# The order of ScalarE's work in each step of an expert loop, and the place of SiLU's table load

## The chip, the cores and the metric

The kernel runs on one core of a Trainium2 chip. The metric is the device time in microseconds (us) from start to end of one execution; lower is better. Engines are named as in the profile: PE is TensorE's matmuls, PEld its weight loads, DVE is VectorE, ACT is ScalarE, POOL is GpSimd, SP is SyncE, which issues the loads of weights.

## The reference

A model of 256 tokens of width 1024 in fp32. First come two hybrid layers, then two layers that mix pooling and attention; the first of these ends in a dense SwiGLU, the second in a mixture of 8 experts. The change lies in the experts:

```python
def swiglu(h, wg, wu, wd):
    return (jax.nn.silu(h @ wg) * (h @ wu)) @ wd

def moe_swiglu(h, w_router, wg, wu, wd):
    xt = h.reshape(-1, D)
    logits = (xt @ w_router).astype(jnp.float32)
    top_v, top_i = lax.top_k(logits, TOP_K)
    gates = jax.nn.softmax(top_v, axis=-1)
    gate = jnp.sum(jax.nn.one_hot(top_i, N_EXPERTS) * gates[..., None], axis=1)
    y = jnp.zeros_like(xt)
    for e in range(N_EXPERTS):
        y = y + gate[:, e:e + 1] * swiglu(xt, wg[e], wu[e], wd[e])
```

wg and wu are 1024 x 3584 for each expert, wd is 3584 x 1024. A final rmsnorm follows.

## The kernel before, in words

**Split products.** An fp32 weight is used as two numbers that TensorE multiplies faster, a high part and a low part. SyncE loads a chunk of weights of 1 MiB (128 x 2048 fp32) into one of 6 buffers `raw`. ScalarE copies it to `whi` (the high part, two instructions of 128x1024, function `act_hi_moe`). VectorE subtracts, `wlo = raw - whi` (`dve_lo_moe`, two instructions). TensorE then multiplies with both. There are 4 buffers `whi` (`HIGH`), 3 buffers `wlo` (`SPLIT`) and 6 `raw` (`RAW`). A `raw` buffer is free once its low part is made (`lo_ready`), and SyncE waits for that before it issues the load of the chunk six places on.

**Jobs, pairs and steps.** Tokens are gathered by expert into jobs. The kernel works on pairs of jobs: a heavy one (up to 128 tokens) and a light one (up to 64, its high and low parts side by side). A job has 42 chunks: for each block of 1024 columns 4 chunks of the gate's weights (`g`) and 4 of the value's (`u`), three times, then a block of 512 columns with 2 and 2, then 14 chunks of the down weights (`d`). A pair so has 84 steps, one chunk each, in an order written out by hand (`FIRST_ORDER` for the first pair, 12 steps of the heavy job alone, then heavy and light by turns; `PAIR_ORDER` for the others). Four pairs run here, three written out and one in a loop with a trip count from the router. A heavy step is 12 matmuls of 128x512, a light one 8.

**What a step asks of ScalarE.** At step `i` it makes the high part of chunk `i + 4`, which may start when TensorE has finished step `i` (`split_used`) and the chunk has landed. At some steps it also reads accumulators out of PSUM:
- where the heavy gate ends (`plan.gate[HEAVY_JOB]`): SiLU of both banks into `act_h`, line 1342 (in the trace the tile is called xlo_plain_sb). The first bank may be read from the middle of the step on, since a heavy step works on its first half of columns first:

```python
if p % 2 == 0 and q < WIDE_BLOCKS:
    act.wait_ge(h_half_ps, 2 * WIDE_BLOCKS * j + 2 * q + 1)
else:
    act.wait_ge(split_used, number(AT_MOE, i + 1, PER, j))
```

- where the light gate or the light value ends (`plan.gate[LIGHT_JOB]`, `plan.value[LIGHT_JOB]`): a copy into `row_l`, lines 1355 and 1367;
- where the down product ends (`plan.y_out`, function `y_read`): the high part of the result into `yghi`, line 1322. VectorE then makes `yglo` (line 2093), and TensorE scatters both back to the tokens (`scatter`, lines 2631 and 2632).

The accumulators have one set of banks for each job, used in turn for gate and value. So TensorE may not start a value's first chunk before the gate is read (`heavy_bank_free` waits for `hg_silu`, half by half; `light_waits` for `lg_copied`), nor the next gate before the value is read. The heavy job's value is multiplied with SiLU's result by VectorE, then transposed by TensorE and split again (`turn_h`); the light job's rows are folded by small matmuls (line 2728) and go through SiLU and the split (`silu_l`, `split_l`) later.

**The order on ScalarE** is that of the program, an engine runs its instructions in turn. In `pair` of `scalar_program` each step first issues `act_hi_moe(act, i + HIGH, j)`, then the readouts, with `y_read` last, save in the loop's last step, where it is first. ScalarE's table of functions is loaded by an instruction ACT_TABLE_LOAD that the compiler places before the first function of another set; Exp is used in the router, SiLU next in step 3 of the first pair, and Copy is between them.

Of the kernel before, what the change touches and what calls it, by code (L numbers as in the profile page):

```python
# [22 lines left out]
ACT = mybir.ActivationFunctionType  # L23
# [105 lines left out]
HIGH = 4  # L129
KC = 4  # L130
NC = 512
# [62 lines left out]
HEAVY_JOB, LIGHT_JOB = 0, 1  # L194
# [18 lines left out]
def blocks_of(q):  # L213

    return (2 * q, 2 * q + 1) if q < WIDE_BLOCKS else (2 * q,)


def group_cols(q):

    return slice(q * WIDE, q * WIDE + NC * len(blocks_of(q)))  # L220
# [51 lines left out]
PER = len(PAIR.steps)  # L272
# [11 lines left out]
AT_MOE = AT_MIX1 + len(MIXER)  # L284
# [61 lines left out]
def build(nc, A):  # L346

    ctx = ExitStack()
    with ctx:
        def sb(name, shape, dt=F32, stack=ctx):  # L350
            name = f"{name}_sb"
            return stack.enter_context(nc.sbuf_tensor(name, shape, dt))

        def sem(name):
            return ctx.enter_context(nc.semaphore(name))
# [11 lines left out]
        con = sb("con", [PART, N_KEPT])  # L367
# [3 lines left out]
        stat = sb("stat", [PART, 40])  # L371
# [36 lines left out]
        ahi2 = sb("ahi2", [PART, D_FFE], F32R, stack=moe)  # L408
# [3 lines left out]
        row_l = sb("row_l", [PART, WIDE], stack=before_y)  # L412
# [56 lines left out]
        split_used = sem("split_used")  # L469
# [82 lines left out]
        hT_ps = sem("hT_ps")  # L552
        h_hi = sem("h_hi")
        h_lo = sem("h_lo")
        lg_copied = sem("lg_copied")
        lu_copied = sem("lu_copied")
        lgT_ps = sem("lgT_ps")
# [65 lines left out]
        def act_h_of(p):  # L623

            return act_h[:, 4 * (p % 2):4 * (p % 2) + 4, :]

        def in_blocks(bank):

            return bank.rearrange("p (k n) -> p k n", n=PART)
# [5 lines left out]
        def h_tp(q):  # L635

            return tp[:, 0:2, :].rearrange("p b n -> p (b n)")[:, 0:NC * len(blocks_of(q))]

        def l_banks(q, which):

            if q < WIDE_BLOCKS:
                return acc[:, LIGHT_JOB, :, :].rearrange("p b n -> p (b n)")
            return acc[:, LIGHT_JOB, "gu".index(which), :]
# [75 lines left out]
        def number(c0, i, per=0, l=0):  # L719
            return c0 + i + per * l  # L720
# [9 lines left out]
        def moe_raw(i, l):  # L730

            if first(l) and i in AHEAD:
                return raw_ahead[AHEAD.index(i)]
            return raw[ring_at(i, l) % RAW]

        def wait_landed_moe(engine, i, l):

            if first(l) and i in AHEAD:
                engine.wait_ge(ahead_landed[AHEAD.index(i)], 16)
            else:  # L740
                r = ring_at(i, l)
                engine.wait_ge(raw_landed[r % RAW], landed(AT_MOE, r, PER, l))
# [39 lines left out]
        def first(j):  # L782

            return isinstance(j, int) and j == 0
# [250 lines left out]
        def act_hi_moe(act, i, l):  # L1035

            wait_landed_moe(act, i, l)
            if not first(l) or i >= HIGH:
                act.wait_ge(split_used, number(AT_MOE, i - HIGH + 1, PER, l))
            for c in range(0, KC, KC // 2):  # L1040
                nc.scalar.activation(whi_moe[i % HIGH][:, c:c + KC // 2, :], moe_raw(i, l)[:, c:c + KC // 2, :],  # L1041
                                     ACT.Copy).then_inc(hi_ready, 1)
# [43 lines left out]
        def scalar_program(act):  # L1086
# [207 lines left out]
            nc.scalar.activation(xnhi[:, :, :], xw[:, :, :], ACT.Copy).then_inc(xn_hi, 1)  # L1294
            act.wait_ge(lg_ready, 1)
            nc.scalar.activation(lg[:, :, :], lg[:, :, :], ACT.Exp).then_inc(expl_ready, 1)

            def gathered(n, r, cols):
                act.wait_ge(xg_ps, ROUNDS * n + r + 1)
                a, b = cols  # L1300
                hi_ps, lo_ps = (bank.rearrange("p (c n) -> p c n", c=2) for bank in xg_tp(n, r))
                nc.scalar.activation(xhi[:, 2 * r:2 * r + 2, a:b], hi_ps[:, :, a:b], ACT.Copy).then_inc(xg_hi, 1)
                if a < PART:
                    last = nc.scalar.activation(xlo[:, 2 * r:2 * r + 2, 0:PART], lo_ps[:, :, 0:PART], ACT.Copy)
                if b > PART:
                    last = nc.scalar.activation(xhi[:, 2 * r:2 * r + 2, PART + LIGHT:2 * PART],
                                                lo_ps[:, :, PART:PART + LIGHT], ACT.Copy)
                last.then_inc(xg_lo, 1)
# [7 lines left out]
            def y_read(j, i, b):  # L1316

                act.wait_ge(split_used, number(AT_MOE, i + 1, PER, j))
                if not first(j) or b:
                    act.wait_ge(scat_ps, 2 * j + b)  # L1320
                for h in range(2):
                    nc.scalar.activation(yghi[:, h * NC:(h + 1) * NC], acc[:, b, h, :], ACT.Copy).then_inc(yg_hi, 1)

            def pair(j, plan):
                done = GROUPS * j
                for i in range(PER):
                    y_first = i == PER - 1 and not isinstance(j, int)
                    if y_first:
                        y_read(j, i, plan.y_out[i])

                    act_hi_moe(act, i + HIGH, j)

                    if i in plan.gate[HEAVY_JOB]:
                        q = plan.gate[HEAVY_JOB][i]
                        if not first(j) or q:
                            act.wait_ge(hT_ps, done + q)
                        for p in blocks_of(q):
                            if p % 2 == 0 and q < WIDE_BLOCKS:
                                act.wait_ge(h_half_ps, 2 * WIDE_BLOCKS * j + 2 * q + 1)
                            else:  # L1340
                                act.wait_ge(split_used, number(AT_MOE, i + 1, PER, j))
                            nc.scalar.activation(act_h_of(p), in_blocks(h_bank(p, "g")), ACT.Silu).then_inc(hg_silu, 1)  # L1342
                    if i in plan.turn_h:
                        q = plan.turn_h[i]
                        act.wait_ge(hT_ps, done + q + 1)
                        nc.scalar.activation(ahi2[:, group_cols(q)], h_tp(q), ACT.Copy).then_inc(h_hi, 1)

                    if i in plan.gate[LIGHT_JOB]:
                        q = plan.gate[LIGHT_JOB][i]
                        act.wait_ge(split_used, number(AT_MOE, i + 1, PER, j))  # L1350
                        if q:
                            act.wait_ge(luT_ps, done + q)
                        elif not first(j):
                            act.wait_ge(scat_ps, 2 * j)
                        nc.scalar.activation(row_l[:, 0:NC * len(blocks_of(q))], l_banks(q, "g"),
                                             ACT.Copy).then_inc(lg_copied, 1)
                    if i in plan.silu_l:
                        q = plan.silu_l[i]
                        act.wait_ge(lgT_ps, done + q + 1)
                        if not first(j) or q:  # L1360
                            act.wait_ge(l_lo, done + q)
                        nc.scalar.activation(l_act_of(q), l_tp(q, "g"), ACT.Silu).then_inc(l_silu, 1)
                    if i in plan.value[LIGHT_JOB]:
                        q = plan.value[LIGHT_JOB][i]
                        act.wait_ge(split_used, number(AT_MOE, i + 1, PER, j))
                        act.wait_ge(lgT_ps, done + q + 1)
                        nc.scalar.activation(row_l[:, 0:NC * len(blocks_of(q))], l_banks(q, "u"),
                                             ACT.Copy).then_inc(lu_copied, 1)
                    if i in plan.split_l:
                        q = plan.split_l[i]  # L1370
                        act.wait_ge(l_act, done + q + 1)
                        nc.scalar.activation(l_parts(q)[0], l_blocks(l_act_of(q)), ACT.Copy).then_inc(l_hi, 1)

                    if first(j) and i in LIGHT_GATHER:
                        gathered(1, LIGHT_GATHER[i], (PART, PART + LIGHT))
                    if i == plan.back:
                        act.wait_ge(back_ps, j + 1)
                        nc.scalar.activation(backT[:, :, :, :].rearrange("p b t n -> p (b t n)"), tp[:, 3, :],
                                             ACT.Copy).then_inc(back_ready, 1)
                    if i in plan.gather:  # L1380
                        gathered(j + 2, plan.gather[i], (0, PART + LIGHT))
                    if i in plan.y_out and not y_first:
                        y_read(j, i, plan.y_out[i])

            for j in range(WRITTEN_OUT):
                if j == WRITTEN_OUT - 1:
# [1495 lines left out]
```

## Time and profile before

| | us |
|---|---|
| median of 3 runs | 1595.25 (1595.08 to 1595.58) |
| the profiled execution's own time | 1596.01 |
| its span, first to last instruction | 1594.2 |
| TensorE busy | 1523.5 (96%) |
| VectorE busy | 1279.2 (80%) |
| ScalarE busy | 1099.6 (69%) |
| mean granted TensorE clock | 0.985 of full |

The expert part runs from about 667 us to the end. "Busy" counts instructions at work. Matmuls overlap: one of 128x512 lasts 0.39 us in the trace, but the next starts 0.23 us after it, so the spacing of starts is what to read. "Idle before, releaser" names what ended an engine's wait. The DMA share is the time of all packets over that of 16 DMA engines; it can be a little over 1 because packets of one engine overlap.

### The profile page before, as it was taken

Reading aid. Unit: us, or ns where it says so; the run is one execution under the profiler, and the core shown is the slowest. Engines: PE = TensorE matmul, PEld = TensorE weight load, DVE = VectorE, ACT = ScalarE, POOL = GpSimd, SP = SyncE. Lnnn points to the kernel's source line nnn. Section 1 sums busy time; section 2 is a strip of 40 time slices with the busy share of each in tenths; the row PEclk is TensorE's granted clock in tenths of the full one; section 3 lists DMA queues with packets and bytes.
Section 4 is the critical chain, followed back from the end, with each engine's and each line's share of the span. In section 5 each row is a group of like instructions: output and inputs, shape, how many; then the busy total and the mean of one; then the engine's idle time right before and its main releaser. Section 6 shows DMA issues by size and latency. Waiting matters only on the chain.

```text
span 1594.2 us, 20968 instructions
## 1 busy us (share of the span) xinstructions
PE 1523.5 (96%) x7379; PEld 1261.2 (79%) x7379; DVE 1279.2 (80%) x1519; ACT 1099.6 (69%) x1417; POOL 120.3 (8%) x242
## 2 busy tenths in 40 slices
PE   6999999999999999689999999999999999999995
PEld 5788788888888888668888787788778887778884
DVE  5686586566545547669999999999999999999998
ACT  3664565554444455368888888888888888788886
POOL 3433431101000000100000000000000000000000
PEclk9999999999999999799999999999999999999998
DMA  9646443526545654359999999999999999999995
GB/s 325 215 144 178 168 140 137 191 100 192 172 159 191 211 178 165 118 212 347 383 408 405 386 393 403 386 385 400 385 407 394 395 373 409 377 408 386 384 393 231
DMA packets 153702, 463.70 MB, mean 291 GB/s; under 512 B 7950, under 2 KB 12444, under 8 KB 153468
## 3 DMA queue, kind: packets, MB, share of 16 engines
q1 hardware_dynamic: 150656, 454.85, 76.6%
q0 software_dynamic: 1888, 5.31, 1.3%
q10 hardware_dynamic: 1052, 2.19, 0.4%
q8 instruction: 59, 0.97, 0.3%
q14 instruction: 47, 0.39, 0.1%
HBM read 461.27 MB, written 1.05 MB: 290 GB/s over the span
## 4 chain that ended last, share of the span: by engine, by line
PE 79%; DVE 7%; ACT 5%; issue 3%; DMA 3%; DVEq 2%; SPq 0%; ACTq 0%
PE ps L2199 8%; PE ps L2667 8%; PE ps L2200 8%; PE ps L2201 8%; PE ps L2669 8%; PE ps L2668 8%; PE ps L2682 7%; PE ps L2683 7%; DVE wlo_sb L1430 4%; ACT whi_sb L1041 3%; PE ps L2728 3%; DMA raw_sb<-w_in 2%; PE ps L2617 1%; PE ps L2245 1%; PE ps L2777 1%
## 5 line engine op out<-in xcount | busy, mean ns | idle before, releaser
L1430 DVE TENSOR_TENSOR wlo_sb<-raw_sb,whi_sb 128x1024 fp32r<-128x1024 f32 x666 | 770.9, 1217 | 49.9 <-PE ps L2669 40.6
L1041 ACT ACTIVATE whi_sb<-raw_sb 128x1024 fp32r<-128x1024 f32 x668 | 663.6, 1052 | 151.7 <-PE ps L2669 109.1
L1421 DVE TENSOR_TENSOR wlo_sb<-raw_sb,whi_sb 128x1024 fp32r<-128x1024 f32 (+2 forms) x198 | 230.1, 1203 | 143.8 <-ACT whi_sb L1032 142.7
L1032 ACT ACTIVATE whi_sb<-raw_sb 128x1024 fp32r<-128x1024 f32 (+2 forms) x198 | 192.2, 1022 | 161.9 <-PE ps L2201 131.3
L2199 PE MATMUL ps<-whi_sb,xlo_sb 128*128 128x512 f32 (+2 forms) x544 | 212.8, 391 | 4.3 <-DVE xlo_sb L1469 4.3
L2200 PE MATMUL ps<-wlo_sb,xhi_sb 128*128 128x512 f32 (+2 forms) x544 | 208.6, 384 | 0.0
L2201 PE MATMUL ps<-whi_sb,xhi_sb 128*128 128x512 f32 (+2 forms) x544 | 208.5, 383 | 0.0
L2667 PE MATMUL ps<-whi_sb,xlo_sb 128*128 128x512 f32 x448 | 180.3, 402 | 14.3 <-ACT xlo_plain_sb L1342 12.5
L2682 PE MATMUL ps<-whi_sb,xhi_sb 128*128 128x512 f32 x448 | 180.4, 403 | 6.1 <-DVE wlo_sb L1430 3.5
L2669 PE MATMUL ps<-whi_sb,xhi_sb 128*128 128x512 f32 x448 | 176.2, 393 | 0.0
L2668 PE MATMUL ps<-wlo_sb,xhi_sb 128*128 128x512 f32 x448 | 175.9, 393 | 0.0
L2683 PE MATMUL ps<-wlo_sb,xhi_sb 128*128 128x512 f32 x448 | 175.1, 391 | 0.0
L2199 PEld LDWEIGHTS ps<-whi_sb,xlo_sb 128*128 128x128 f32 x544 | 103.2, 190 | 25.9 <-DVE wlo_sb L1421 4.5
L2201 PEld LDWEIGHTS ps<-whi_sb,xhi_sb 128*128 128x128 f32 x544 | 103.1, 189 | 19.4
L2200 PEld LDWEIGHTS ps<-wlo_sb,xhi_sb 128*128 128x128 f32 x544 | 103.2, 190 | 18.7 <-issue 0.5
L2667 PEld LDWEIGHTS ps<-whi_sb,xlo_sb 128*128 128x128 f32 x448 | 84.8, 189 | 37.0 <-issue 11.9
L2682 PEld LDWEIGHTS ps<-whi_sb,xhi_sb 128*128 128x128 f32 x448 | 84.1, 188 | 28.6 <-DVE wlo_sb L1430 5.2
L2669 PEld LDWEIGHTS ps<-whi_sb,xhi_sb 128*128 128x128 f32 x448 | 84.9, 189 | 18.9
L2668 PEld LDWEIGHTS ps<-wlo_sb,xhi_sb 128*128 128x128 f32 x448 | 85.1, 190 | 16.9
L2683 PEld LDWEIGHTS ps<-wlo_sb,xhi_sb 128*128 128x128 f32 x448 | 84.3, 188 | 16.1
L2682 PE MATMUL ps<-whi_sb,alT_sb 128*128 128x512 f32 x224 | 89.9, 401 | 2.3 <-DVE wlo_sb L1430 2.1
L2667 PE MATMUL ps<-whi_sb,alo_sb 128*128 128x512 f32 x224 | 89.9, 401 | 0.0
(390 smaller groups left out, 2099.6 us busy)
## 6 DMA issues: line engine op xcount, KB each, us to landing
raw_sb<-moe_wg SPq DMA_DIRECT2D x115, 1024.0 KB, 8.1
raw_sb<-moe_wd SPq DMA_DIRECT2D x112, 1024.0 KB, 8.0
raw_sb<-moe_wu SPq DMA_DIRECT2D x110, 1024.0 KB, 7.8
raw_sb<-w_in SPq DMA_DIRECT2D x40, 1024.0 KB, 5.2
raw_sb<-w_out SPq DMA_DIRECT2D x16, 1024.0 KB, 5.0
raw_sb<-ffn_wg SPq DMA_DIRECT2D x10, 1024.0 KB, 5.1
raw_sb<-ffn_wu SPq DMA_DIRECT2D x10, 1024.0 KB, 5.1
raw_sb<-ffn_wd SPq DMA_DIRECT2D x10, 1024.0 KB, 5.0
```

Of the source, the lines that this page charges most:

```text
L1032: nc.scalar.activation(whi[i % SPLIT][:, c:c + k // 2, 0:n], raw[i % RAW][:, c:c + k // 2, 0:n], ACT.Copy).then_inc(hi_ready, 1)
L1041: nc.scalar.activation(whi_moe[i % HIGH][:, c:c + KC // 2, :], moe_raw(i, l)[:, c:c + KC // 2, :], ACT.Copy).then_inc(hi_ready, 1)
L1421: op = V.tensor_tensor(wlo[i % SPLIT][:, c:c + k // 2, 0:n], raw[i % RAW][:, c:c + k // 2, 0:n], whi[i % SPLIT][:, c:c + k // 2, 0:n], ALU ...
L1430: op = V.tensor_tensor(wlo[i % SPLIT][:, c:c + KC // 2, :], moe_raw(i, l)[:, c:c + KC // 2, :], whi_moe[i % HIGH][:, c:c + KC // 2, :], AL ...
L2199: mm(out, lo, whi[i % SPLIT][:, c, 0:chunk.n], start=first, stop=False)
L2200: mm(out, hi, wlo[i % SPLIT][:, c, 0:chunk.n], start=False, stop=False)
L2201: op = mm(out, hi, whi[i % SPLIT][:, c, 0:chunk.n], start=False, stop=last)
L2667: mm(o, lo, whi_moe[i % HIGH][:, w, :], start=first, stop=False)
L2668: mm(o, hi, wlo[i % SPLIT][:, w, :], start=False, stop=False)
L2669: op = mm(o, hi, whi_moe[i % HIGH][:, w, :], start=False, stop=last)
L2682: mm(o, both, whi_moe[i % HIGH][:, w, :], start=first, stop=False)
L2683: op = mm(o, both, wlo[i % SPLIT][:, w, :], start=False, stop=last)
```

## The change

In `pair` of `scalar_program`, all readouts of accumulators (`y_read`, SiLU of the heavy gate, the copies of the light gate and the light value) now stand ahead of `act_hi_moe` in each step. `turn_h`, `silu_l`, `split_l` and the rest stay behind it. Behind the router's Exp a SiLU of one column, whose result nobody reads, is added. No wait of TensorE, VectorE or SyncE changes.

```diff
--- before.py
+++ after.py
@@ -1294,6 +1294,7 @@
             nc.scalar.activation(xnhi[:, :, :], xw[:, :, :], ACT.Copy).then_inc(xn_hi, 1)
             act.wait_ge(lg_ready, 1)
             nc.scalar.activation(lg[:, :, :], lg[:, :, :], ACT.Exp).then_inc(expl_ready, 1)
+            nc.scalar.activation(stat[:, 6:7], con[:, 0:1], ACT.Silu)
 
             def gathered(n, r, cols):
                 act.wait_ge(xg_ps, ROUNDS * n + r + 1)
@@ -1324,12 +1325,8 @@
             def pair(j, plan):
                 done = GROUPS * j
                 for i in range(PER):
-                    y_first = i == PER - 1 and not isinstance(j, int)
-                    if y_first:
+                    if i in plan.y_out:
                         y_read(j, i, plan.y_out[i])
-
-                    act_hi_moe(act, i + HIGH, j)
-
                     if i in plan.gate[HEAVY_JOB]:
                         q = plan.gate[HEAVY_JOB][i]
                         if not first(j) or q:
@@ -1340,11 +1337,6 @@
                             else:
                                 act.wait_ge(split_used, number(AT_MOE, i + 1, PER, j))
                             nc.scalar.activation(act_h_of(p), in_blocks(h_bank(p, "g")), ACT.Silu).then_inc(hg_silu, 1)
-                    if i in plan.turn_h:
-                        q = plan.turn_h[i]
-                        act.wait_ge(hT_ps, done + q + 1)
-                        nc.scalar.activation(ahi2[:, group_cols(q)], h_tp(q), ACT.Copy).then_inc(h_hi, 1)
-
                     if i in plan.gate[LIGHT_JOB]:
                         q = plan.gate[LIGHT_JOB][i]
                         act.wait_ge(split_used, number(AT_MOE, i + 1, PER, j))
@@ -1354,18 +1346,26 @@
                             act.wait_ge(scat_ps, 2 * j)
                         nc.scalar.activation(row_l[:, 0:NC * len(blocks_of(q))], l_banks(q, "g"),
                                              ACT.Copy).then_inc(lg_copied, 1)
+                    if i in plan.value[LIGHT_JOB]:
+                        q = plan.value[LIGHT_JOB][i]
+                        act.wait_ge(split_used, number(AT_MOE, i + 1, PER, j))
+                        act.wait_ge(lgT_ps, done + q + 1)
+                        nc.scalar.activation(row_l[:, 0:NC * len(blocks_of(q))], l_banks(q, "u"),
+                                             ACT.Copy).then_inc(lu_copied, 1)
+
+                    act_hi_moe(act, i + HIGH, j)
+
+                    if i in plan.turn_h:
+                        q = plan.turn_h[i]
+                        act.wait_ge(hT_ps, done + q + 1)
+                        nc.scalar.activation(ahi2[:, group_cols(q)], h_tp(q), ACT.Copy).then_inc(h_hi, 1)
+
                     if i in plan.silu_l:
                         q = plan.silu_l[i]
                         act.wait_ge(lgT_ps, done + q + 1)
                         if not first(j) or q:
                             act.wait_ge(l_lo, done + q)
                         nc.scalar.activation(l_act_of(q), l_tp(q, "g"), ACT.Silu).then_inc(l_silu, 1)
-                    if i in plan.value[LIGHT_JOB]:
-                        q = plan.value[LIGHT_JOB][i]
-                        act.wait_ge(split_used, number(AT_MOE, i + 1, PER, j))
-                        act.wait_ge(lgT_ps, done + q + 1)
-                        nc.scalar.activation(row_l[:, 0:NC * len(blocks_of(q))], l_banks(q, "u"),
-                                             ACT.Copy).then_inc(lu_copied, 1)
                     if i in plan.split_l:
                         q = plan.split_l[i]
                         act.wait_ge(l_act, done + q + 1)
@@ -1379,8 +1379,6 @@
                                              ACT.Copy).then_inc(back_ready, 1)
                     if i in plan.gather:
                         gathered(j + 2, plan.gather[i], (0, PART + LIGHT))
-                    if i in plan.y_out and not y_first:
-                        y_read(j, i, plan.y_out[i])
 
             for j in range(WRITTEN_OUT):
                 if j == WRITTEN_OUT - 1:
```

## Rows read from the trace of the kernel before

**Rows 1.** The page: busy time, share and instructions of each engine.
```profile
PE 1523.5 (96%) x7379; PEld 1261.2 (79%) x7379; DVE 1279.2 (80%) x1519; ACT 1099.6 (69%) x1417; POOL 120.3 (8%) x242
```

**Rows 2.** Busy by stretch: length, each engine's busy (x), clock, DMA share, GB/s.
```profile
680.00:720.00 40.00, 34.98 (x161) 29.11 (x162) 25.80 (x30) 24.83 (x35) 0.00 (x0) 0.91 0.53 189
740.00:1560.00 820.00, 801.23 (x3785) 656.96 (x3785) 778.75 (x728) 686.30 (x780) 0.00 (x0) 1.00 1.02 393
982.34:1025.02 42.68, 41.57 (x201) 34.27 (x200) 40.37 (x37) 36.12 (x39) 0.00 (x0) 1.00 1.01 389
```

**Rows 3.** The weights' DMA queue, 740 to 1560 us: packets, MB, share of 16 engines.
```profile
q1 hardware_dynamic: 91679, 321.86, 101.2%
```

**Rows 4.** DMA queues, 1160 to 1200 us, and their total rate.
```profile
DMA packets 4259, 16.43 MB, mean 411 GB/s; under 512 B 254, under 2 KB 254, under 8 KB 4257
...
q1 hardware_dynamic: 4257, 16.40, 102.3%
```

**Rows 5.** ScalarE in order of time, step 3: start, us, instruction, [idle before].
```profile
676.35 2.01 ACT L1041 ACTIVATE whi_sb<-ahead_in_alo_sb 128x1024 fp32r<-128x1024 f32 x2 [0.71 <-PE ps L2669]
679.10 2.01 ACT L1041 ACTIVATE whi_sb<-ahead_in_alT_sb 128x1024 fp32r<-128x1024 f32 x2 [0.74 <-PE ps L2669]
681.13 1.28 ACT L1342 ACT_TABLE_LOAD   x1
682.42 1.08 ACT L1342 ACTIVATE xlo_plain_sb<-ps 128x512 f32<-128x512 f32 x2
```

**Rows 6.** TensorE in order of time, steps 3 and 11.
```profile
678.61 0.40 PE L2669 MATMUL ps<-whi_sb,xhi_sb 128*128 128x512 f32 x1
683.16 0.66 PE L2667 MATMUL ps<-whi_sb,xlo_sb 128*128 128x512 f32 x1 [4.16 <-ACT xlo_plain_sb L1342]
...
686.88 0.40 PE L2667 MATMUL ps<-whi_sb,xlo_sb 128*128 128x512 f32 x1
...
710.78 0.61 PE L2617 MATMUL ps<-pick_sb,xnlo_sb 128*128 128x192 f32 x4
713.24 0.47 PE L2667 MATMUL ps<-whi_sb,xlo_sb 128*128 128x512 f32 x1 [1.86 <-ACT xlo_plain_sb L1342]
...
714.02 0.63 PE L2667 MATMUL ps<-whi_sb,xlo_sb 128*128 128x512 f32 x1
...
717.43 0.39 PE L2669 MATMUL ps<-whi_sb,xhi_sb 128*128 128x512 f32 x1
```

**Rows 7.** The stretch behind step 11, columns as in rows 2.
```profile
714.00:717.40 3.40, 3.40 (x9) 2.65 (x8) 0.00 (x0) 0.00 (x0) 0.00 (x0) 0.50 1.00 396
```

**Rows 8.** ScalarE in the router stage.
```profile
656.08 0.22 ACT L1296 ACTIVATE lg_sb<-lg_sb 128x16 f32<-128x16 f32 x1 [0.49 <-DVE lg_sb L1952]
662.26 0.38 ACT L1302 ACTIVATE xhi_sb<-ps 128x256 fp32r<-128x256 f32 x1 [5.96 <-PE ps L2617]
```

**Rows 9.** Waits, 720 to 1575 us: total us, times, longest us.
```profile
PE ps L2667 <- ACT xlo_plain_sb L1342: 6.5, 7, 1.2
...
PE ps L2631 <- DVE yglo_sb L2093: 4.7, 3, 1.7
PEld ps L2682 <- ACT row_l_sb L1355: 4.2, 7, 0.7
...
PEld ps L2667 <- ACT xlo_plain_sb L1342: 2.8, 2, 1.7
...
PEld ps L2682 <- ACT row_l_sb L1367: 1.4, 2, 0.7
```

**Rows 10.** Groups by line, 900 to 1560 us: busy us, mean ns.
```profile
L1355 ACT ACTIVATE row_l_sb<-ps 128x1024 f32<-128x1024 f32 x9 | 9.2, 1018 | 0.0
```

**Rows 11.** One chunk's high part on ScalarE, its low part on VectorE.
```profile
979.65 2.01 ACT L1041 ACTIVATE whi_sb<-raw_sb 128x1024 fp32r<-128x1024 f32 x2 [0.72 <-PE ps L2683]
...
982.34 4.63 DVE L1430 TENSOR_TENSOR wlo_sb<-raw_sb,whi_sb 128x1024 fp32r<-128x1024 f32 x4 [0.39 <-PE ps L2669]
```

## The prediction

> **What bounds the kernel now.** I read the page first: TensorE is 96% busy, VectorE 80%, ScalarE 69% [rows 1]. ScalarE is the least busy of the three, so a new order on it can help only where another engine waits for it. Then the table by stretch, because the change lies in the expert part alone. From 740 to 1560 us TensorE is busy 801 of 820 us, VectorE 779 and ScalarE 686, and the DMA share is 1.02 at 393 GB/s [rows 2]. The reader should see that three resources are near full together. One period of 16 steps in the middle of a pair (982.34 to 1025.02) says the same: 42.68 us, VectorE busy 40.37.
>
> The DMA question decides most of what follows, so I compared a calm stretch with the whole. Over 740:1560 the weights' queue, q1, took 101.2% of 16 engines' time [rows 3]. In 1160:1200, where nothing disturbs it, it took 102.3%, and all queues together moved 411 GB/s [rows 4]. I read 102.3% as "never empty". Over the 820 us the queue was then empty for about (102.3 - 101.2)/102.3 = 1.1%, which is 9 us. The rest of the difference between 393 and 411 GB/s is packets that took longer, not missing requests. So the 16 steps cost the DMA at least 16 x 1.0486 MB / 411 GB/s = 40.8 us, and VectorE 40.4 us, against the 42.68 that they take. TensorE's waits set the pace in a calm period, and the transfers are less than 2 us behind.
>
> **The start of the experts.** Between 676 and 720 us it is otherwise. The stretch 680:720 is not DMA-bound, its DMA share is 0.53 [rows 2]. Here TensorE waits for ScalarE alone. In step 3 the heavy job's gate ends, and ScalarE has two things in its queue: the high part of chunk 7 (679.10, 2.01 us), then SiLU, and before SiLU its table load (681.13, 1.28 us) [rows 5]. TensorE's last matmul before it starts at 678.61 and the next at 683.16, where 0.23 us is the usual spacing: 4.55 - 0.23 = 4.32 us lost. From there to 686.88 nine spacings take 3.72 us instead of 9 x 0.23 = 2.07: the granted clock has dropped to its half level, and 1.65 us more are lost [rows 6]. The same happens in step 11: the gathers end at 710.78 + 0.61 = 711.39, the next matmul starts at 713.24 (1.86 us idle), and from 714.02 to 717.43 eight spacings take 3.41 us instead of 1.83, at a granted clock of 0.50, 1.58 us more [rows 6, 7].
>
> **The change part by part.**
>
> *Readouts first, heavy gate.* The SiLU of the gate's first half waits for a semaphore that TensorE gives in the middle of the step, and ScalarE is free by 676.35 + 2.01 = 678.36, before the step ends near 678.9. In the new order it reads that half at once (0.54 us), done by the end of the step. The second half follows while TensorE works on the value's first half. So in steps 3 and 11 the wait goes wholly: 4.32 + 1.86 = 6.18 us. The two stretches at half clock began after these waits. I take them to go too: 1.65 + 1.58 = 3.23 us. Sum: 9.4 us. Bounds: 6.2 if the clock falls anyway, 9.4 if not. I take 9.4 because nothing else idles TensorE there. What hangs on TensorE (step 9's end frees the ring slot for chunk 15, and so on) moves with it, the transfers too, so it isn't given back.
>
> *The SiLU table.* One load of 1.28 us leaves that wait (it is in the 4.32) and goes behind Exp, where ScalarE is idle for 5.96 us before the first gathered read [rows 8]. The dummy activation works on one column; the nearest row is Exp's 16 columns at 0.22 us, which I take. Both cost nothing while those 5.96 us stand; without them it would be 1.5 us on the path. In the row SiLU starts 0.01 us behind the load [rows 5]. The Trainium skill, page "ScalarE: Activation LUTs", section "What ACT_TABLE_LOAD costs", gives 1283 ns and a drain of about 1380 ns. The load agrees, the drain doesn't show here. By the page 2.66 us would move, still inside the idle time.
>
> *Readouts first, at the 14 later places of a pair* (4 SiLU, 4 and 4 copies, 2 of y). From 720 to 1575 us TensorE waits for SiLU 6.5 us (7 times) and its weight loads 2.8 (2 times); for the light gate's copy 4.2 us (7), the light value's 1.4 (2), and for the low part of y, whose high part ScalarE makes late, 4.7 (3) [rows 9]. Sum: 19.6 us. The new order removes nearly all of these. But now the other limits count. TensorE, set free, asks for chunks at 40.4 us per 16 (VectorE's work), and the DMA gives them at 40.8 or more. The transfers can't be compressed by more than their empty time, 9 us. Earlier slots fill part of it; some of it lies at the change of pairs, where VectorE is behind with the scattered sums and no readout helps. Bounds: 0 and 9; I take 5, as the new order also lets y out earlier at that very place.
>
> *What is late instead.* Each high part that follows a readout comes about 1.0 us later (a 128x1024 copy takes 1018 ns, and the two halves of y are taken as two of SiLU's, 1.08) [rows 5, 10]. Queued behind it is VectorE's low part of the same chunk. The nearest pair of rows: ScalarE starts a chunk's high part at 979.65, so its first half is ready about 980.7. VectorE starts on that chunk at 982.34, and what it waited for is TensorE, not ScalarE [rows 11]. Cover: 1.6 us against a delay of 1.0. Hence 0, with up to 0.5 us each if the cover shrinks as the pipeline tightens. No new semaphore wait stands ahead of the high part except those of the step just ended, for which it waits itself. SP's queue and POOL's aren't touched.
>
> **Sum.** 9.4 + 5 = 14.4 us. The profiled execution took 1596.01 us (span 1594.2), 0.8 over the median of 1595.25; I subtract from the median: 1580.9, so 1581.
>
> **The rivals.**
>
> *A: the queues aren't the limit.* If the DMA serves faster as soon as it is asked, all 19.6 us come back: 1595.2 - 9.4 - 19.6 = 1566. For it: the landed chunks wait for ScalarE most of the time, since it waits for TensorE in nearly every calm step. Against: the share of 101.2%. Chance 0.10. The Trainium skill, page "DMA: Bandwidth & Descriptors", table under "Measured", has 425 GB/s for 16 MB. By it 16 steps could take 39.5 us and this rival would be likelier; the highest calm rate here is 411.
>
> *B: the queues take everything in the steady part.* Only the start gains: 1595.2 - 9.4 = 1586. For it: 393 GB/s in every long stretch whatever the engines do. Against: 1% of empty time exists and long gaps between requests make it. Chance 0.22.
>
> *C: slower.* The delayed high parts reach TensorE. Per pair the readouts put ahead add 3.5 x 1.08 for SiLU, twice 3.5 x 1.02 for the copies (the last block is a half) and 2 x 1.08 for y, about 13 us, 52 in four pairs. The place is VectorE's low part at the tightest steps, after the light copies. It decides when more than 14.4/52, over a quarter, of the delay gets through. At a half it is 26 - 14.4 = 12 us slower: 1607. Against it stands the cover of 1.6 us. Chance 0.03.
>
> *D: the change doesn't do what it says.* The load is made again at the first SiLU, or the clock falls without a wait, and the queues take the rest: the gain shrinks to 6.2 - 1.3 = 5 us or below, 1590 to 1595. Chance 0.05.
>
> *The forecast*, 1578 to 1584: 0.60.
>
> **How the numbers follow.** The range of 8 in 10 has to reach B with its own spread, but not A, C or D: 1575 to 1588. 0.2% (3.2 us) is about what a measurement of this kernel can tell from no change. Faster: the forecast, A, B and most of D, 0.94. Same: 0.03 from D. Slower: C, 0.03.
>
> **What the changed profile would show.** No ACT_TABLE_LOAD at L1342, one after Exp. No TensorE gap over 0.3 us behind steps 3 and 11, and no half-clock stretch there. SiLU and the copies gone from the list of TensorE's waits. Chunks landing at the same 411 GB/s in calm stretches, with the mean over the experts near 395 and the share nearer 102.3% of 16 engines, ScalarE waiting for landings more often. I am wrong if that rate rises to 400 or more (A), if the share stays while ScalarE's waits only change their name (B), or if VectorE's waits for whi_sb or TensorE's for wlo_sb grow by 10 us (C).

## The result, and the profile after

The changed kernel takes 1567.55 us (median of 4 runs, 1567.03 to 1568.74) against 1595.16 for the kernel before (4 runs): a ratio of 0.9829, 95% interval 0.9812 to 0.9846. It is 27.6 us faster. Forecast were 1581 and a range of 1575 to 1588, so the gain is nearly twice the one predicted, and the time lies under the range. It is near the time of rival A (1566), which had a chance of 0.10.

The changed kernel by stretch, columns as in [rows 2]; the third row is one period of 16 steps in the middle of a pair:

```profile
680.00:720.00 40.00, 40.00 (x198) 33.39 (x198) 34.51 (x38) 30.90 (x42) 0.00 (x0) 1.00 0.73 260
740.00:1540.00 800.00, 793.15 (x3772) 655.30 (x3771) 775.24 (x726) 684.98 (x779) 0.00 (x0) 1.00 1.02 402
968.73:1009.74 41.01, 41.01 (x202) 34.43 (x201) 40.13 (x38) 35.83 (x39) 0.00 (x0) 1.00 1.03 406
```

In 680:720 TensorE now has no gap (it was busy 34.98 of 40 us before) and its clock stays whole (1.00 against 0.91). From 740 us on it is busy 793 of 800 us, and the transfers run at 402 GB/s where they ran at 393. A period of 16 steps takes 41.01 us instead of 42.68, with TensorE busy all the time. The queue of the weights and all queues together:

```profile
DMA packets 91502, 321.68 MB, mean 402 GB/s; under 512 B 4897, under 2 KB 4897, under 8 KB 91445
...
q1 hardware_dynamic: 91445, 320.97, 102.1%
```

The queue's share of 16 engines' time is 102.1%, from 101.2% [rows 3]: 0.9% more for 2.3% more bytes a second (the stretches are 740:1540 here and 740:1560 there; in 740:1540 the kernel before has 393 GB/s too).

ScalarE in the router stage and in step 3 (start, length, instruction, idle before):

```profile
657.34 0.22 ACT L1296 ACTIVATE lg_sb<-lg_sb 128x16 f32<-128x16 f32 x1 [0.50 <-DVE lg_sb L1950]
657.58 1.28 ACT L1297 ACT_TABLE_LOAD   x1
658.87 0.21 ACT L1297 ACTIVATE stat_sb<-con_sb 128x1 f32<-128x1 f32 x1
663.52 0.38 ACT L1303 ACTIVATE xhi_sb<-ps 128x256 fp32r<-128x256 f32 x1 [4.45 <-PE ps L2615]
...
678.02 2.01 ACT L1041 ACTIVATE whi_sb<-ahead_in_alo_sb 128x1024 fp32r<-128x1024 f32 x2 [0.71 <-PE ps L2667]
679.94 0.58 ACT L1339 ACTIVATE xlo_plain_sb<-ps 128x512 f32<-128x512 f32 x1
680.72 0.60 ACT L1339 ACTIVATE xlo_plain_sb<-ps 128x512 f32<-128x512 f32 x1 [0.20 <-PE ps L2667]
681.21 2.01 ACT L1041 ACTIVATE whi_sb<-ahead_in_alT_sb 128x1024 fp32r<-128x1024 f32 x2
```

The table load stands behind Exp, in idle time: 4.45 us are left before the gathered rows. In step 3 the first SiLU runs from 679.94, before the step's end, the second from 680.72, and the high part of chunk 7 follows. TensorE at the same place:

```profile
680.28 0.40 PE L2667 MATMUL ps<-whi_sb,xhi_sb 128*128 128x512 f32 x1
680.66 0.47 PE L2665 MATMUL ps<-whi_sb,xlo_sb 128*128 128x512 f32 x1
680.97 0.40 PE L2666 MATMUL ps<-wlo_sb,xhi_sb 128*128 128x512 f32 x1
```

From the last matmul of the gate (680.28) to the first of the value (680.66) there are 0.38 us, where there were 4.55 [rows 6]. The waits from 720 to 1575 us (total, times, longest):

```profile
PE ps L2680 <- DVE wlo_sb L1428: 5.4, 4, 1.9
PEld ps L2680 <- DVE wlo_sb L1428: 4.9, 5, 1.8
...
PEld ps L2665 <- DVE wlo_sb L1428: 2.3, 4, 0.6
...
PEld ps L2629 <- ACT xhi_sb L1303: 0.5, 1, 0.5
...
DVE wlo_sb L1428 <- ACT whi_sb L1041: 0.2, 1, 0.2
```

SiLU, the copies of the light job and the low part of y, 19.6 us in [rows 9], are gone. What is left is VectorE's low part of the weights, at the change of pairs. (The list also has 1.1 and 1.7 us for y at line 2828. That is the last stage of the kernel, which now starts before 1575 us.)

### The profile page after: what moved, and what is told of

It is laid out like the page before. It is cut to its first block, busy times and chain, and to the rows that moved or that the text cites. A ratio compares the mean times of both kernels' runs of the same rounds, so it can differ in the third digit from the quotient of the medians.

```text
span 1566.9 us, 20980 instructions
## 1 busy us (share of the span) xinstructions
PE 1515.3 (97%) x7379; PEld 1260.1 (80%) x7379; DVE 1277.8 (82%) x1519; ACT 1099.0 (70%) x1418; POOL 118.2 (8%) x242
## 4 chain that ended last, share of the span: by engine, by line
PE 83%; DVE 9%; DMA 3%; issue 2%; DVEq 2%; ACT 1%; SPq 0%; ACTq 0%
PE ps L2665 9%; PE ps L2667 9%; PE ps L2666 9%; PE ps L2197 9%; PE ps L2199 8%; PE ps L2198 8%; PE ps L2680 8%; PE ps L2681 7%; DVE wlo_sb L1428 5%; PE ps L2726 3%; DMA raw_sb<-w_in 2%; PE ps L2615 1%; DMA raw_sb<-moe_wg 1%; PE ps L2775 1%; PE ps L2243 1%
## 5 line engine op out<-in xcount | busy, mean ns | idle before, releaser
L2199 PEld LDWEIGHTS ps<-whi_sb,xhi_sb 128*128 128x128 f32 x544 | 103.1, 189 | 19.5
```

Of the source, the lines that this page charges most:

```text
L2199: op = mm(out, hi, whi[i % SPLIT][:, c, 0:chunk.n], start=False, stop=last)
```

## The experiments

Two theories about the surplus of the gain over the forecast. Theory 1: TensorE's waits for ScalarE came back one for one; the transfers had more room than their busy share showed. Theory 2: the transfers were near full as predicted, and the surplus has another source (the start, or y at the change of pairs). Medians are set against those of the kernel before on the same chip; the ratio has its 95% interval.

**e1_table: the table load alone.**

```diff
             nc.scalar.activation(lg[:, :, :], lg[:, :, :], ACT.Exp).then_inc(expl_ready, 1)
+            nc.scalar.activation(stat[:, 6:7], con[:, 0:1], ACT.Silu)
```

> The kernel before with SiLU's table load behind Exp and nothing else. Theory 1 (TensorE's waits for ScalarE come back one for one, the transfers had more room than their busy share showed) and theory 2 (the transfers give back at most some 5 us in the steady part, the surplus comes from elsewhere) both expect 1.3 us less, 1593.9: the wait in step 3 falls from 4.3 us to 3.0, which is still long, so the half-clock stretch behind it stays. If the clock doesn't fall behind 3.0 us, 1.65 us more.

1592.31 us against 1594.61, ratio 0.9982 (0.9973 to 0.9991): 2.3 us less by the medians. The waits of TensorE in 676:720 and two stretches of the trace (the clock is the third figure from the end):

```profile
PE ps L2668 <- ACT xlo_plain_sb L1343: 4.9, 2, 3.0
```

```profile
670.00:711.30 41.30, 36.44 (x180) 30.35 (x179) 31.71 (x34) 28.06 (x37) 0.00 (x0) 1.00 0.56 195
711.30:714.70 3.40, 3.40 (x10) 2.63 (x9) 0.00 (x0) 0.23 (x2) 0.00 (x0) 0.50 1.02 405
```

The longer wait is 3.0 us, as expected. The clock did not fall behind it (1.00 from 670 to 711.3), so the 1.65 us of the half-clock stretch came on top of the 1.3. Together that is 2.95 us, inside the interval of the times (1.4 to 4.3 us). It did fall behind step 11, where the wait was the shorter one (4.9 - 3.0 = 1.9 us).

**e2_heavy_first: SiLU of the heavy gate first, nothing else.**

```diff
-                    act_hi_moe(act, i + HIGH, j)
-
                     if i in plan.gate[HEAVY_JOB]:
...
                             nc.scalar.activation(act_h_of(p), in_blocks(h_bank(p, "g")), ACT.Silu).then_inc(hg_silu, 1)
+
+                    act_hi_moe(act, i + HIGH, j)
```

> The kernel before with only SiLU of the heavy gate ahead of the high part. Start: step 3 keeps the table load but reads from the middle of the step, 2.8 us less; step 11 1.9 less; two half-clock stretches 3.2. Steady part: TensorE's waits for SiLU are 6.5 + 2.8 = 9.3 us from 720 us on. Theory 1: 7.9 + 9.3 = 17 us, 1578. Theory 2: 7.9 + at most 3 = 11 us, 1584.

1583.03 against 1594.61, ratio 0.9930 (0.9917 to 0.9944): 11.6 us less. That is theory 2's number, and taken alone it would have misled. The waits from 720 to 1575 us show why:

```profile
PEld ps L2683 <- ACT row_l_sb L1356: 7.7, 7, 1.6
PE ps L2683 <- ACT row_l_sb L1356: 7.2, 7, 1.2
```

The light gate's copy cost 4.2 us at the weight loads [rows 9] and 1.9 at the matmuls in the kernel before, whose line is

```profile
PE ps L2682 <- ACT row_l_sb L1355: 1.9, 7, 0.4
```

Here it costs 7.7 and 7.2. ScalarE in order of time, in the middle of a pair of e2:

```profile
997.80 1.06 ACT L1340 ACTIVATE xlo_plain_sb<-ps 128x512 f32<-128x512 f32 x2
998.75 3.89 ACT L1041 ACTIVATE whi_sb<-raw_sb 128x1024 fp32r<-128x1024 f32 x4
1002.54 1.01 ACT L1356 ACTIVATE row_l_sb<-ps 128x1024 f32<-128x1024 f32 x1
```

The heavy gate ends one step ahead of the light one. SiLU, put first, delays that step's high part, and the light copy stands behind it and behind its own step's high part (the four instructions between). 5.3 us at the matmuls went there, of the 6.5 that the matmuls had waited for SiLU.

**e3_light_first: the copies of the light gate and value first.** Both blocks moved ahead of `act_hi_moe`:

```diff
+                    if i in plan.gate[LIGHT_JOB]:
...
+                    if i in plan.value[LIGHT_JOB]:
...
                     act_hi_moe(act, i + HIGH, j)
```

> The kernel before with only the copies of the light gate and light value ahead of the high part. Waits 4.2 + 1.4 us. Theory 1: 5.6 us less, 1589.6. Theory 2: 2 us less or none, 1593 to 1595.

1587.29 against 1594.61, ratio 0.9952 (0.9938 to 0.9966): 7.3 us less, 5.4 to 9.9 by the interval. Theory 1's 5.6 us is inside, near its lower end; theory 2 with 2 us or none is outside.

**e4_y_first: y first.**

```diff
-                    y_first = i == PER - 1 and not isinstance(j, int)
+                    y_first = i in plan.y_out
```

> The kernel before with only y read first. Waits for the low part of y 4.7 us, at the change of pairs, where ScalarE waits for landed chunks. Theory 1: 4.7 us less, 1590.5. Theory 2: chunks land no earlier there, 1 us or none, 1594 to 1595. A third theory, that the surplus over the waits comes from here, since y is what VectorE's backlog at the change of pairs begins with: 8 us or more.

1591.29 against 1594.61, ratio 0.9978 (0.9969 to 0.9987): 3.3 us less, 2.1 to 4.9 by the interval. Theory 1's 4.7 is inside, theory 2's 1 us is not, and the third theory's 8 us isn't either.

**e5_start_only: the new order in the heavy job's lead alone, with the table load.**

```diff
-                    act_hi_moe(act, i + HIGH, j)
+                    early = first(j) and i < LEAD
+                    if not early:
+                        act_hi_moe(act, i + HIGH, j)
...
+                    if early:
+                        act_hi_moe(act, i + HIGH, j)
                     if i in plan.turn_h:
```

> The kernel before with the table load moved and SiLU of the heavy gate read first in the first 12 steps of the experts alone (the heavy job's lead); every later step as before. It isolates the first term of the sum. If that term was right: 9.4 us less, 1585.5, and the later part, from 720 us on, takes as long as before. If the surplus lies at the start: 14 us less or more.

1586.57 against 1595.25, ratio 0.9935 (0.9915 to 0.9956): 8.7 us less by the medians, 7.0 to 13.6 by the interval. By stretch:

```profile
680.00:720.00 40.00, 40.00 (x200) 33.65 (x199) 34.88 (x38) 31.07 (x41) 0.00 (x0) 1.00 0.73 264
740.00:1540.00 800.00, 781.44 (x3694) 640.32 (x3693) 759.27 (x710) 670.11 (x763) 0.00 (x0) 1.00 1.02 393
```

The start is as in the changed kernel (40.00 busy, clock 1.00) and the later part as before (393 GB/s). So the prediction's first term, 9.4 us, holds, and the surplus lies in the later part. In the traces the 12 steps of the lead take 9.44 us less than before here, and 9.45 us less in the changed kernel.

**e6_transfers_alone and e7_longer_light: what the transfers can do, and what their share shows.** e6 leaves the products of the low weights out and makes only the second half of each low part, so its result isn't the reference's. e7 counts the light job's low product twice, which changes the result too.

```diff
+                if c == 0:
+                    continue
...
-                    mm(o, hi, wlo[i % SPLIT][:, w, :], start=False, stop=False)
...
-                    mm(o, both, whi_moe[i % HIGH][:, w, :], start=first, stop=False)
-                    op = mm(o, both, wlo[i % SPLIT][:, w, :], start=False, stop=last)
+                    op = mm(o, both, whi_moe[i % HIGH][:, w, :], start=first, stop=last)
```

> The changed kernel with the products of the low weights left out (8 matmuls a heavy step, 4 a light one) and the second half of each low part alone made, so that the transfers alone limit the expert part. Theory 1, the transfers had room: they land at 405 GB/s or more, above the 393 of before and the 402 of the changed kernel, in 740 to 1500 us. Theory 2, the queues were full and 393 to 402 is what the memory gives with its disturbances: at most 402. The queue's share of 16 engines' time should be the 102.3% of the calm stretch.

One run each, 1545.15 us for e6. TensorE is busy 582 of 760 us in it, VectorE 427 and ScalarE 658. Its queues from 740 to 1500 us, and the time from issue to landing in us (last figure):

```profile
DMA packets 88095, 308.79 MB, mean 406 GB/s; under 512 B 4701, under 2 KB 4701, under 8 KB 88053
...
q1 hardware_dynamic: 88053, 308.29, 102.7%
...
raw_sb<-moe_wd SPq DMA_DIRECT2D x109, 1024.0 KB, 11.8
```

With the products cut down the transfers run at 406 GB/s for 760 us on end, disturbances included. The kernel before had 394 in the same stretch. Room there was, 3.0%, which is some 24 us of 820.

```diff
+                    mm(o, both, wlo[i % SPLIT][:, w, :], start=False, stop=False)
                     op = mm(o, both, wlo[i % SPLIT][:, w, :], start=False, stop=last)
```

> The kernel before with 4 more matmuls in each light step (the low product counted twice), so that TensorE alone sets the pace at about 16 steps in 50 us, 335 GB/s. This asks what the queue's share shows when the transfers are surely not the limit. If the share means what the prediction took it for, it falls with the rate, to 102.3 x 335/411 = 83%. If it stays over 90% the share counts time in which a packet or an engine waits for the next request, and that was the prediction's error.

e7 takes 1734.77 us, and its queues show:

```profile
DMA packets 73241, 259.10 MB, mean 341 GB/s; under 512 B 3948, under 2 KB 3948, under 8 KB 73194
...
q1 hardware_dynamic: 73194, 258.48, 94.1%
...
raw_sb<-moe_wd SPq DMA_DIRECT2D x84, 1024.0 KB, 5.2
raw_sb<-moe_wg SPq DMA_DIRECT2D x82, 1024.0 KB, 6.7
```

TensorE sets the pace (busy 756.8 of 760 us) at 341 GB/s, and the share is 94.1%. If it followed the rate from the calm stretch (102.3% at 411 GB/s, [rows 4]) it would be 85%. Nine points are busy time that the rate doesn't account for. The same is seen in the kernel before, in a stretch just behind a change of pairs (1360 to 1380 us, busy tenths and GB/s in slices of 0.5 us):

```profile
DMA  9967889999978999779999999999789999979998
GB/s 418 385 279 238 188 246 352 401 401 426 369 303 328 385 401 328 238 328 385 418 418 410 418 418 426 426 352 229 172 311 360 393 393 410 279 279 410 410 360 262
DMA packets 1810, 6.98 MB, mean 349 GB/s; under 512 B 107, under 2 KB 107, under 8 KB 1810
...
q1 hardware_dynamic: 1810, 6.98, 96.8%
```

At 349 GB/s, 15% under the calm rate, the share is 96.8%, only 5% under. The fifth slice moved 188 GB/s and the sixth 246, under half and 60% of the calm rate, and both count as 80% busy.

Where that busy time sits can be read from the single packets of 4 KiB in the traces. Their median length is 159 to 162 ns in every kernel, but some last over 200 ns, 430 to 460 ns on average:

| | GB/s | of them over 200 ns | what these add, share of the 4 KiB packets' time | loads under way |
|---|---|---|---|---|
| e7, 740:1500 | 341 | 6.9% | 11.5% | 1 to 3 |
| before, 740:1560 | 393 | 1.9% | 3.5% | 2 to 4 |
| after, 740:1540 | 402 | 0.8% | 1.4% | 2 to 4 |
| e6, 740:1500 | 406 | 0.2% | 0.3% | 4 or 5 |

In e7 they crowd 1.0 to 2.0 us behind the issue of a load: 16 to 18% of the packets that start there are long, against 2 to 3% in the first 1.0 us. So the surplus of busy time is a few long packets, and from kernel to kernel there are more of them the fewer loads are under way. What such a packet waits for isn't shown.

**e8_all_first: the other readouts ahead too.** `turn_h`, `silu_l` and `split_l` also stand before `act_hi_moe`.

```diff
-                    act_hi_moe(act, i + HIGH, j)
-
                     if i in plan.turn_h:
...
                         nc.scalar.activation(l_parts(q)[0], l_blocks(l_act_of(q)), ACT.Copy).then_inc(l_hi, 1)
+                    act_hi_moe(act, i + HIGH, j)
```

> The changed kernel with the other readouts ahead of the high part too: the turned activations' high part, SiLU of the light gate and the light split. In the changed kernel TensorE doesn't wait for these. Theory 1: nothing to come back, 1566 to 1569; or slower by a few us, because the high part comes 2 us late in some steps. Theory 2 has no other view.

1567.76 against 1595.25, ratio 0.9826 (0.9806 to 0.9847), the same as the changed kernel. No wait was there to come back. By the traces 58 of 332 high parts start over 0.5 us later than in the changed kernel, against the end of a step of TensorE, 8 of them over 1.5 us, and it costs nothing that the times show.

**e9_without_table: the changed kernel without the dummy SiLU.**

```diff
-            nc.scalar.activation(stat[:, 6:7], con[:, 0:1], ACT.Silu)
```

> The changed kernel without the table load behind Exp. Theory 1 (waits come back one for one): in step 3 the load of 1.28 us then stands before SiLU's first half, which ends at about 680.2 on the scale of before instead of 678.9, so TensorE waits 1.3 to 1.5 us: 1.3 to 1.5 us slower than the changed kernel, 1569; 1.6 more, 1570.6, if the clock falls to its half level behind that wait.

1569.13 against 1594.93, ratio 0.9838 (0.9825 to 0.9852): 1.6 us over the changed kernel's median. The two intervals overlap, so the times alone don't show it. The trace has the wait, in 676:720:

```profile
PE ps L2664 <- ACT xlo_plain_sb L1338: 1.4, 1, 1.4
```

It is 1.4 us, once, and the clock stays at 1.00 behind it. The table load is worth that in the new order, and no more.

**e10_light_behind: the changed kernel with the light job's copies behind again.**

```diff
+                    act_hi_moe(act, i + HIGH, j)
+
                     if i in plan.gate[LIGHT_JOB]:
...
-                    act_hi_moe(act, i + HIGH, j)
-
                     if i in plan.turn_h:
```

> The changed kernel with the copies of the light gate and value behind the high part again. Alone, ahead of an otherwise old order, these two gave 7.3 us. If the parts simply add, this one is 7 us over the changed kernel, 1575. If SiLU read first makes the light copy later (with SiLU alone first TensorE's weight loads waited 7.7 us for that copy instead of 4.2), it is 10 us or more over, 1578. Theory 2 expects 2 us or less.

1579.73 against 1594.93, ratio 0.9906 (0.9891 to 0.9921): 12.2 us over the changed kernel. The waits are those of e2:

```profile
PEld ps L2680 <- ACT row_l_sb L1350: 7.7, 7, 1.6
PE ps L2680 <- ACT row_l_sb L1350: 7.2, 7, 1.2
```

The light copies, worth 7.3 us alone, are worth 12.2 on top of SiLU. It is what e2 lost.

**All of them step by step.** TensorE's semaphore for a finished step gives the end of each of the 336 steps in every trace. This is how much longer (+) or shorter (-) the steps took than in the trace of the kernel before, in us:

| | lead, 12 steps | 7 steps with a stop for SiLU | 14 with one for a light copy | 5 at the end of y | all others |
|---|---|---|---|---|---|
| after | -9.4 | -8.4 | -6.3 | -3.9 | -0.9 |
| e2, SiLU | -8.0 | -8.4 | +5.8 | -2.0 | -0.9 |
| e3, light copies | 0.0 | -0.5 | -6.3 | -0.7 | -0.8 |
| e4, y | 0.0 | -0.5 | -0.1 | -4.5 | 0.0 |
| e5, lead alone | -9.4 | -0.5 | 0.0 | -0.5 | +0.2 |
| e10, no light copies | -9.4 | -8.4 | +5.6 | -4.1 | -0.7 |

Up to 1 us, 2 us at y, also appears where nothing was changed. Each readout put first takes its own steps' waits away, by nearly the same amount in every kernel. The one effect across places is that of SiLU on the light copies: +5.8 in e2 and +5.6 in e10, instead of -6.3.

## Why the prediction was wrong

*The start, 9.4 us.* Right, in place and size (e5: 8.7 by the medians). Both half-clock stretches went with the waits.

*The table load.* Right: hidden behind Exp, in 1.28 + 0.21 us of 5.96.

*The later places.* Here the prediction failed. The places of the waits were right, and the step "the transfers can't be compressed by more than their empty time, 9 us" cut them to 5. Its premise was "I read 102.3% as never empty", and that the rest of the difference between 393 and 411 GB/s was "packets that took longer, not missing requests". Packets did take longer (1.9% of them over 200 ns), but long packets come with few loads under way and not with full queues: e7, at a pace that TensorE alone sets, has 6.9% of them and a share of 94.1%. e6 shows how fast the transfers can be, 406 GB/s. What came back in the later part is 27.6 - 9.4 = 18.2 us by the medians (19.5 by the steps of the two traces), against 5 in the sum and at most 9.

*The 19.6 us of waits.* The total is close to what came back, partly by luck. It adds idle times of PE and PEld, which can be one and the same stop. The 2.8 us of PEld for SiLU are the two stops at 1417.47 and 1460.16, and the 6.5 us of PE have both already:

```profile
1417.47 0.19 PEld L2667 LDWEIGHTS ps<-whi_sb,xlo_sb 128*128 128x128 f32 x1 [1.67 <-ACT xlo_plain_sb L1342]
1417.48 0.50 PE L2667 MATMUL ps<-whi_sb,xlo_sb 128*128 128x512 f32 x1 [1.25 <-ACT xlo_plain_sb L1342]
```

So SiLU was counted at 9.3 us, where the steps gave back 8.4. The copies were counted at 5.6, where they gave 6.3, and y at 4.7, where it gave 3.9. The idle time of PE is less than a stop costs, since a matmul's 0.39 us in the trace cover part of the gap between starts that are 0.23 us apart. Theory 1 holds, place by place, for what a stop costs by the steps, and rival A's 1566 is so near partly because the errors cancel.

The prediction's own figures disagreed, and it didn't notice. It had 42.68 us for a period and 40.8 for the transfers in it, 1.9 us of room. Seven periods from 720 us on have both stops ([rows 9], 7 times for SiLU), which makes 13 us, more than the 9 that it allowed. The period now takes 41.01 us: 1.67 x 7 = 11.7 us. The rest of the gain lies at the other light copies and at y.

*The single places* give by the medians 11.6 + 7.3 + 3.3 + 2.3 = 24.5 us alone and 27.6 together. SiLU alone first gave less than its waits, the light copies on top of it gave more, because they stand in one queue one step apart. And the half-clock stretch behind step 3 is in two of these parts, e1 and e2.

*What is late instead, 0 us.* Right; even e8's further delay, over 1.5 us for 8 high parts, costs nothing that shows.

*The rivals.* A was the case, and its sign came: a rate of 400 GB/s or more (402). The argument held against it was the share. B is out by the time and by the gains from 720 us on. C is out by its own signs: VectorE's wait for whi_sb is 0.2 us, and PE's for wlo_sb is 6.5 us as before (5.6 + 0.9, now 5.4 + 1.1). The figure of the Trainium skill, page "DMA: Bandwidth & Descriptors", section "Measured", 425 GB/s for 16 MB, is for loads issued from GpSimd and isn't reached here: 406 over 309 MB in e6, 411 in a calm stretch. It pointed the right way all the same.

Left open is what the long packets wait for, and why the clock falls behind some waits and not behind others. None of the complete kernels here is faster than the changed one. In the expert part e6 leaves it 402 to 406 GB/s, 1% of 800 us or 8 us, and in the calm period TensorE has no gap left.

## What to carry to other kernels

An engine that is only 69% busy can still hold up the busiest one by the order of its queue: issue first what somebody waits for, and behind it what is needed steps later. A busy share of the DMA near or over 100% is no proof that the transfers are the limit. The time from issue to landing tells more: 5.2 to 6.7 us with TensorE in the lead (e7), 8 before, 8.5 to 9.0 after, 11.8 with the transfers in the lead (e6). And a stop of TensorE is read from the starts of its matmuls, not from the idle times of PE and PEld added up. Parts of such a change that share a queue have to be tried together, since one of them alone can move the wait to the next.

## What the runs showed of the hardware

The busy share of the DMA engines follows the rate only weakly: 94.1% at 341 GB/s, 101.2% at 393, 102.1% at 402, 102.7% at 406. The difference is in packets of 4 KiB that last over 200 ns instead of 159 to 162, 6.9% of them at 341 GB/s and 0.2% at 406.

TensorE's clock fell to its half level for 3.4 us behind idle times of 4.2 us (step 3, 4.3 by the starts) and 1.9 us (step 11) in the kernel before, but not behind one of 3.0 us in step 3 of e1, in which the one of 1.9 us still had it. Nor did it fall behind 1.4 us in step 3 of e2 and e9. At the first change of pairs an idle time of 1.9 to 2.1 us is in the trace of every complete kernel. The clock fell behind it in the kernel before, e4, e5 and e10, and not in the changed kernel, e1, e2, e3, e8 and e9. The length of an idle time alone doesn't tell.
